# Final norm and first modulated norm in one chain of sums, in a two-stack transformer kernel

## The reference

```python
def rms_norm(x, g):
    return x * rsqrt(mean(x * x) + EPS) * g

x_end_of_first_stack:
x = rms_norm(x, final_norm)
each_layer_of_the_second_stack:
h = rms_norm_2(x, norm1) * (1.0 + scale1) + shift1
proj = h @ w_in
...
x = x + gate1 * mix
h2 = rms_norm_2(x, norm2) * (1.0 + scale2) + shift2
```

## Time and profile before

| | us |
|---|---|
| timed runs, median of 3 | 3476.75 |
| lowest and highest | 3476.37, 3479.42 |
| profiled execution | 3465.51 |
| its span | 3463.7 |
| TensorE, matmul records busy in it | 3345.2 |
| VectorE, ScalarE, GpSimd busy | 1544.0, 1214.1, 748.0 |

### The profile page before, as it was taken

The page is one execution under the profiler, slowest core; times in us unless marked ns, Lnnn a source line. Parts: engine busy times, 40 slices in busy tenths (PEclk is TensorE's granted clock), DMA queues, the critical chain, the costliest instruction groups (busy, mean ns, idle before and its releaser), DMA issues.

```text
span 3463.7 us, 40850 instructions
## 1 busy us (share of the span) xinstructions
PE 3345.2 (97%) x15998; PEld 2602.6 (75%) x15998; DVE 1544.0 (45%) x1953; ACT 1214.1 (35%) x1657; POOL 748.0 (22%) x390
## 2 busy tenths in 40 slices
PE   7999999999999999999999999989999998999999
PEld 5888776578887888876578887746788877568887
DVE  4444545545535543334543334455433345453333
ACT  4332311543323332335643323245322232552221
POOL 6677500057767740000000000030000002100000
PEclk9999999999999999999999999999999999999999
DMA  6544421145444542221033323201223331013322
GB/s 198 158 146 155 136 74 49 37 135 149 147 152 144 155 115 96 97 74 49 25 85 97 98 97 79 72 25 37 73 97 97 96 91 61 1 49 97 97 97 73
DMA packets 324130, 330.02 MB, mean 95 GB/s; under 512 B 29616, under 2 KB 284720, under 8 KB 323632
## 3 DMA queue, kind: packets, MB, share of 16 engines
q1 hardware_dynamic: 309424, 278.02, 26.0%
q0 software_dynamic: 14592, 50.44, 4.6%
HBM read 326.27 MB, written 2.15 MB: 95 GB/s over the span
## 4 chain that ended last, share of the span: by engine, by line
PE 47%; DVE 2%; ACT 1%; issue 1%; DVEq 0%; ACTq 0%
PE ps L353 18%; PE ps L569 15%; PE ps L408 2%; PE ps L549 2%; PE ps L822 1%; PE ps L849 1%; PE ps L859 1%; PE ps L489 1%; PE ps L460 1%; PE ps L377 1%; PE ps L369 1%; PE ps L1493 1%; PE ps L829 0%; ACT w_hi L302 0%; PE ps L446 0%
## 5 line engine op out<-in xcount | busy, mean ns | idle before, releaser
L306 DVE TENSOR_TENSOR w_lo<-raw,w_hi 128x2048 fp32r<-128x2048 f32 x247 | 609.2, 2466 | 573.3 <-ACT w_hi L302 572.9
L353 PE MATMUL ps<-h_hi,w_hi 128*128 128x512 f32 x2064 | 805.8, 390 | 2.6 <-DVE xT L2004 2.6
L353 PE MATMUL ps<-h_lo,w_hi 128*128 128x512 f32 x2064 | 803.1, 389 | 0.0
L353 PE MATMUL ps<-h_hi,w_lo 128*128 128x512 f32 x2064 | 803.0, 389 | 0.0
L302 ACT CAST w_hi<-raw 128x2048 fp32r<-128x2048 f32 x248 | 473.2, 1908 | 924.9 <-PE ps L353 665.6
L569 PE MATMUL ps<-a_hi,w_hi 128*128 128x512 f32 x1344 | 524.0, 390 | 10.7 <-DVE act L1977 6.2
L569 PE MATMUL ps<-a_hi,w_lo 128*128 128x512 f32 x1344 | 523.0, 389 | 0.0
L569 PE MATMUL ps<-a_lo,w_hi 128*128 128x512 f32 x1344 | 522.9, 389 | 0.0
L353 PEld LDWEIGHTS ps<-h_hi,w_hi 128*128 128x128 f32 x2064 | 387.4, 188 | 84.4 <-issue 4.3
L353 PEld LDWEIGHTS ps<-h_lo,w_hi 128*128 128x128 f32 x2064 | 387.4, 188 | 81.0 <-issue 1.0
L353 PEld LDWEIGHTS ps<-h_hi,w_lo 128*128 128x128 f32 x2064 | 387.4, 188 | 80.8
(11 more groups left out here) (284 smaller groups left out, 4006.3 us busy)
## 6 DMA issues: line engine op xcount, KB each, us to landing
raw<-in_ffn_w_in SPq DMA_DIRECT2D x176, 512.0 KB, 5.0
raw<-in_w_ff SPq DMA_DIRECT2D x128, 512.0 KB, 4.1
m_in<-in_w_mod POOLq DMA_DIRECT2D x96, 512.0 KB, 4.2
raw<-in_ffn_w_out SPq DMA_DIRECT2D x88, 512.0 KB, 4.1
raw<-in_hyb_w_in SPq DMA_DIRECT2D x28, 512.0 KB, 4.2
raw<-in_w_in SPq DMA_DIRECT2D x28, 512.0 KB, 4.7
raw<-in_sb_w_in SPq DMA_DIRECT2D x24, 512.0 KB, 4.2
raw<-in_w_out SPq DMA_DIRECT2D x16, 512.0 KB, 4.3
```

The source lines that it names most:

```text
L306: eng.tensor_tensor(w_lo[:, e % 2], raw[:, e % 2], w_hi[:, e % 2].bitcast(F32), ALU.subtract).then_inc(s["w_lo_done"], 1)
L353: mm = pe.matmul(ps[:, bank], wbuf[a][:, e % 2, at:at + P], hbuf[b][:, k], start=(k == 0 and n == 0), stop=(k == KC - 1 and n == 2))
```

## The change

The phase of the final norm is gone. The first modulated norm (layer 0) gets the number of the final norm's weights as `ph[3]` and makes both factors. ScalarE squares each chunk twice, plain into `act[:, i]` and scaled by the final weight into `act[:, 8 + i]`. `pe_two_sums` adds both sets, each into its half of the partitions of bank 1; the fold takes them apart with two columns of `col_d`. VectorE makes the first factor r into `rcol`, then r^2 times the second mean, then from this the second factor, and the product of both into `r_both`. The final weights are multiplied into `gmod`, so that the modulated norm can read the old `xT`. The product `r_both` is broadcast to bank 1 and `rcol` to bank 3. After the last low part VectorE overwrites `xT` with the final norm's result and counts it in `x_final`, on which TensorE waits in step 1 of `nsa_pre` and VectorE before the attention.

In all four modulated norms VectorE reads the broadcast factor in bank 1 and not a copy; ScalarE's copy stays for the deferred norms alone. The fillers are now 3, 16 and 9 in the joined norm, and 3, 7 and 11 in the other three, with none between the sums. The pending split is now cut in halves in the joined norm too. SyncE's wait for x counts only the updates of x.

```diff
@@ -50,7 +50,7 @@
-    ("norms", len(NORMS) * KC), ("col_d", 1), ("ret_gn", 4), ("c", KC), ("b_mod", DEPTH * 48), ("pool_scale", DEPTH * 4),
+    ("norms", len(NORMS) * KC), ("col_d", 3), ("ret_gn", 4), ("c", KC), ("b_mod", DEPTH * 48), ("pool_scale", DEPTH * 4),
...
-    phases.append(("norm", 6, "final"))
-        phases.append(("norm", 7 + 2 * l, (l, 0)))
+        phases.append(("norm", 7 + 2 * l, (l, 0), 6 if l == 0 else None))
...
@@ -372,26 +376,38 @@
             if c.norm == 1 and j == 0:
                 pe.wait_ge(s["consts_loaded"], 16)
-            pe.wait_ge(s["sq_done"], KC * (c.norm - 1) + (4, 4, 6, 8)[j])
+            pe.wait_ge(s["sq_done"], c.sq + (4, 4, 6, 8)[j])
             for o in range(2):
                 mm = pe.matmul(ps[qk_rows(o), 1], C("ones")[:, 0:HD], act[:, 2 * j + o], start=(j == 0), stop=(j == 3),
                                skip_group_check=True)
             if j == 3:
                 mm.then_inc(s["sums_done"], 1)
-
-        def pe_fold(pe, c):
+                c.sq += KC
+
+        def pe_two_sums(pe, c, i):
+
+            pe.wait_ge(s["sq_done"], c.sq + 2 * max(i, 3) + 2)
+            for o in range(2):
+                mm = pe.matmul(ps[qk_rows(o), 1], C("ones")[:, 0:HD], act[:, 8 * o + i], start=(i == 0), stop=(i == KC - 1),
+                               skip_group_check=True)
+            if i == KC - 1:
+                mm.then_inc(s["sums_done"], 1)
+                c.sq += 2 * KC
+
+        def pe_fold(pe, c, col, n):
             pe.wait_ge(s["sums_copied"], c.norm)
             for b in range(TB):
-                mm = pe.matmul(ps[:, 0, b:b + 1], rstd[:, b * P:(b + 1) * P], PR("col_d", 0),
+                mm = pe.matmul(ps[:, 0, n * b:n * b + n], rstd[:, b * P:(b + 1) * P], PR("col_d", col, n),
                                start=(b == 0), stop=(b == TB - 1), skip_group_check=True)
             mm.then_inc(s["ssq_done"], 1)
-        def pe_bcast(pe, c):
-
-            pe.wait_ge(s["norm_chain"], 6 * c.norm)
+        def pe_bcast(pe, c, of=rcol, bank=1, chain=6):
+
+            c.chain += chain
+            pe.wait_ge(s["norm_chain"], c.chain)
             for b in range(TB):
-                mm = pe.matmul(ps[:, 1, b * P:(b + 1) * P], rcol[:, b:b + 1].to_broadcast([P, P]), C("ident"),
+                mm = pe.matmul(ps[:, bank, b * P:(b + 1) * P], of[:, b:b + 1].to_broadcast([P, P]), C("ident"),
                                start=True, stop=True)
             mm.then_inc(s["bcast_done"], 1)
...
@@ -1059,17 +1075,17 @@
...
-                    sp.wait_ge(s["x_ready"], KC * sum(q[0] == "outp" or q[2:] == ("final",) for q in before))
+                    sp.wait_ge(s["x_ready"], KC * sum(q[0] == "outp" for q in before))
...
-                    sp.wait_ge(s["h_lo_done"], KC * sum(q[0] == "norm" and q[2] != "final" for q in before))
+                    sp.wait_ge(s["h_lo_done"], KC * sum(q[0] == "norm" for q in before))
...
-            sp.wait_ge(s["x_ready"], KC * sum(ph[0] == "outp" or ph[2:] == ("final",) for ph in phases))
+            sp.wait_ge(s["x_ready"], KC * sum(ph[0] == "outp" for ph in phases))
...
@@ -1249,22 +1265,26 @@
             for ph in phases:
                 if ph[0] == "norm":
                     c.norm += 1
-                    c.hnorms += ph[2] != "final"
+                    c.hnorms += 1
                     c.deferred = ph[2] is None
-                    c.fresh = ph[2] != "final"
-                    if not c.deferred:
-                        for j in range(3):
+                    c.fresh = True
+                    if ph[3] is not None:
+                        for i in range(KC):
+                            pe_two_sums(pe, c, i)
+                        keep_warm_by_weights(pe, c, 3)
+                        pe_fold(pe, c, 1, 2)
+                        keep_warm_by_weights(pe, c, 16)
+                        pe_bcast(pe, c, r_both, 1, 15)
+                        pe_bcast(pe, c, rcol, 3, 0)
+                        keep_warm_by_weights(pe, c, 9)
+                    elif not c.deferred:
+                        for j in range(4):
                             pe_sums(pe, c, j)
-                        keep_warm_by_weights(pe, c, 4)
-                        pe_sums(pe, c, 3)
                         keep_warm_by_weights(pe, c, 3)
-                        pe_fold(pe, c)
-                        keep_warm_by_weights(pe, c, 9)
+                        pe_fold(pe, c, 0, 1)
+                        keep_warm_by_weights(pe, c, 7)
                         pe_bcast(pe, c)
-                        keep_warm_by_weights(pe, c, 12)
-                    if ph[2] == "final":
-                        c.outs += 1
-                        c.order = range(KC)
+                        keep_warm_by_weights(pe, c, 11)
                 elif ph[0] == "proj":
                     pe_proj(pe, c, len(ph[2]), "T")
                 elif ph[0] == "projT":
...
@@ -1469,6 +1489,7 @@
                 elif ph[0] == "nsa_pre":
                     l, step = ph[1:]
                     if step == 1:
+                        pe.wait_ge(s["x_final"], KC)
                         pe_hn_sum(pe, c, [nbuf[:, 0], nbuf[:, 1]], 0)
                         pe.wait_ge(s["cm_w"], 80 * (l + 1))
...
@@ -1550,7 +1571,10 @@
                             eng.mul(h_hi[:, k], xT[:, k], PR("norms", ph[1] * KC + k)).then_inc(s["h_hi_done"], 1)
                         eng.activation(act[:, i], xT[:, k], ACT.Square).then_inc(s["sq_done"], 1)
-                    parts = c.pending_split and not c.deferred and ph[2] != "final"
+                        if ph[3] is not None:
+                            eng.activation(act[:, 8 + i], xT[:, k], ACT.Square, scale=PR("norms", ph[3] * KC + k)
+                                           ).then_inc(s["sq_done"], 1)
+                    parts = c.pending_split and not c.deferred
                     if c.pending_split and not parts:
                         c.pending_split()
                     c.pending_split = None
@@ -1558,23 +1582,25 @@
                     eng.copy(rstd[:, :], ps[:, 1]).then_inc(s["sums_copied"], 1)
                     if parts:
                         part_hi(eng, c.slab + 1, 0, 2)
-                    eng.wait_ge(s["norm_chain"], 6 * n + 1)
+                    eng.wait_ge(s["norm_chain"], c.chain + 1)
                     eng.activation(small[:, 52:56], small[:, 48:52], ACT.Sqrt).then_inc(s["rms_done"], 1)
+                    if ph[3] is not None:
+                        eng.wait_ge(s["norm_chain"], c.chain + 9)
+                        eng.activation(small[:, 52:56], small[:, 48:52], ACT.Sqrt).then_inc(s["rms_done"], 1)
+                    c.chain += 6 if ph[3] is None else 15
                     if parts:
                         part_hi(eng, c.slab + 1, 1, 2)
-                    eng.wait_ge(s["bcast_done"], n + 1)
-                    eng.copy(rstd[:, :], ps[:, 1]).then_inc(s["rstd_done"], 1)
-                    if ph[2] not in (None, "final"):
+                    if c.deferred:
+                        eng.wait_ge(s["bcast_done"], n + 1)
+                        eng.copy(rstd[:, :], ps[:, 1]).then_inc(s["rstd_done"], 1)
+                    else:
                         for i, k in enumerate(c.order):
                             eng.wait_ge(s["h_full"], KC * (c.hnorms - 6) + i + 1)
                             at = ph[2][0] * 48 + ph[2][1] * KC + k
                             eng.activation(h_hi[:, k], nbuf[:, i % 2], ACT.Identity, bias=mods[:, at:at + 1]
                                            ).then_inc(s["h_hi_done"], 1)
                     c.norm += 1
-                    c.hnorms += ph[2] != "final"
-                    if ph[2] == "final":
-                        c.outs += 1
-                        c.order = range(KC)
+                    c.hnorms += 1
                 elif ph[0] == "proj":
                     def work(j, e, bank, split):
                         q = c.proj + e
...
@@ -1902,40 +1928,51 @@
                     c.pending = None
                     if n == 0:
                         eng.wait_ge(s["consts_loaded"], 16)
-                    parts = c.pending_split and not c.deferred and ph[2] != "final"
+                    parts = c.pending_split and not c.deferred
                     if c.pending_split and not parts:
                         c.pending_split()
                     c.pending_split = None
-                    ms, y, u = small[:, 48:52], small[:, 52:56], small[:, 56:60]
+                    ms, y, u, ss = (small[:, 48 + 4 * a:52 + 4 * a] for a in range(4))
+
+                    def factor(mean, to):
+                        link(eng, eng.tensor_scalar(ms, mean, EPS, None, ALU.add), "norm_chain")
+                        c.roots += 1
+                        eng.wait_ge(s["rms_done"], c.roots)
+                        link(eng, eng.reciprocal(y, y), "norm_chain")
+                        link(eng, eng.tensor_tensor(u, ms, y, ALU.mult), "norm_chain")
```

(50 more changed lines are left out.)

15 lines of the change are left out of this document (10 added, 5 removed).

## The result

| | before | changed |
|---|---|---|
| timed runs, median (count) | 3476.56 (4) | 3453.47 (4) |
| lowest and highest | 3474.76, 3479.42 | 3451.62, 3460.3 |
| ratio, 95% interval | | 0.9936, 0.9919 to 0.9954 |
| profiled execution | 3465.51 | 3452.8 |
| its span | 3463.7 | 3451.0 |

The changed kernel is 0.6% faster: 23.1 us by the medians, 16 to 28 by the interval. The two profiled executions are 12.7 us apart, which is less than their changed places alone account for (17.4 us and one fall of the clock, 1.6); the table behind e1, e2 and e10 shows where the rest went.

The account below looks back on a forecast made before the run. TensorE is 97% busy, so time is won only where it waits or runs fillers, around the modulated norms. Three norms 6.4, joined norm 10.6 and clock 0.8 sum to 17.8 us off the 3476.75 median: 3459.0, range 3454.5 to 3465.5.

Parts of the forecast that it names:

- The joined norm: Final norm joined with first modulated norm: first sum to first projection 17.7 us instead of 28.3, gain 10.6 us.
- last step: In the joined norm, from VectorE's first product to the first projection matmul: 3.89 us.
- Edit 3: Three other norms: VectorE reads the broadcast in bank 1 without ScalarE's copy, gaining 0.62 us each, products no dearer.
- The moved work: Joined norm: halved weight split and VectorE's eight products making x final; 6.6 us fit into 6.91 us of VectorE idle.
- The forecast's clock: TensorE's clock falls before first projections, 1.6 us lost in one of four places, were expected no oftener in the changed kernel.
- Edits 1 and 2: Three other norms: no fillers inside the sums, 1.28 us each; seven fillers instead of nine before the broadcast, 0.23 each.
- Squares: ScalarE's squares in the joined norm: eight pairs of 0.63 + 0.72 us, ending at 2122.4, ahead of TensorE's sums.
- The cover: Joined norm: the squares stay 1.0 us ahead of TensorE, which wants the last pair at 2123.4.
- The 0.8 us for the clock: First projection behind the double norm lost 1.6 us to a lowered clock; middle between 0 and 1.6 regained.
- The clock rival: Fewer fillers let TensorE's clock fall in two to four of the four norms, 1.6 us each: 3463 to 3466; chance 0.22.
- more than summed: Rival: falls of the clock elsewhere become fewer, giving 3453 to 3456 us; chance 0.08.
- The rival of a later wait: Saving eaten by a wait for the weights of the slabs after the norm: about 3476 us; chance 0.05.

Follow-up runs that it names:

- e1: The kernel before, unchanged, run beside itself: ratio 1.0001, median 3473.7 us against 3474.0.
- e2: The changed kernel, unchanged, timed again: 3451.0 us, ratio 0.9947 to the kernel before.
- e10: The changed kernel, unchanged, timed once more beside e9 on the same chip: 3451.7 us, ratio 0.9939 to the kernel before.
- e6: The changed kernel with the old fillers (4 between the sums, 3, 9, 12) back in the three other norms: one execution, 3453.4 us.
- e5: The changed kernel without any filler in the four modulated norms: 3466.9 us, ratio 0.9976 to the kernel before.
- e9: The changed kernel with ScalarE's copy of the broadcast back in the three other norms (same kernel as e7), timed: 3462.5 us, ratio 0.9969 to before.
- e3: The joined norm alone, the three other norms in their old form: 3459.7 us, ratio 0.9962 to the kernel before.
- e4: The kernel before with only the three other norms changed (fillers 3, 7, 11, no copy), double norm kept: 3468.1 us, ratio 0.9990 to before.
- e7: The changed kernel with ScalarE's copy of the broadcast back in the three other norms: an execution of 3453.1 us.

## Why the prediction was right or wrong

**Right, by its own steps.**
- The joined norm: forecast 17.7 us, measured 17.6 in all seven profiled executions that have it with fillers and full-precision sums. Sums 7.06 forecast, 7.09 by the timeline; the two factors 3.60 and 3.58; broadcast to first product 1.33 and 2134.39 - 2133.19 = 1.20; last step 3.89 and 3.88.
- Edit 3 gave 0.62, as summed, with no dearer products.
- The moved work stayed hidden. VectorE's split followed its eight products at once (2152.61), with none of the 6.91 us of idle time left; it came about 1 us late, and TensorE's next slab hid that, as I had allowed. The high split ahead of it was as late, and is in the kernel before too (e1).
- The forecast's clock: no fall in any first projection of the changed kernel in three executions.

**Off in size.**
- Edits 1 and 2: forecast 1.51 us a norm, measured 1.63 (e6). The first is exact (4.93 to 3.65). The second was 0.35 and not 0.23: I let the gain end where the chain's result meets the load, but before, the broadcast's matmuls also stood behind fillers already loaded, and that went too (load to first product or copy 1.19 us, and not 1.33). Hence 12.0 and not 12.2 in each norm, 0.4 us in all.
- Squares: taken at 1.35 us a pair. In the changed kernel a new pair starts every 1.14 us, and the last one takes 2124.05 - 2122.82 = 1.23 from its first start to its end, because the second square starts before the first is over. The cover was 2.6 us, not 1.0. The upper bound by another line's 0.72 us was right for the duration (0.71); I had added durations where ScalarE overlaps neighbours.

**Wrong: the step from the profiled execution to the median ("I take the same 17.8 off the median"), and with it the range.** The stages gave 17.0 and the clock 0.8; the program's own gain is 17.4 by the stages and 18.4 at equal clock, within 1 us of the forecast's 17.8. But I took three timed runs within 3 us of one another for the spread of this kernel, and their median for its level. With 69 runs the spread is 17 us (3464.1 to 3481.2), and the mean 3473.1, 3.6 us below the 3476.75 I started from. The profiled execution I argued from, 11 us below that median, had been the sign of it. The rest of the miss is that the means of 69 and 16 runs lie 20.7 us apart and not 17.8. A median of four runs on either side may stray several microseconds; the measured 23.1 did, and the later ratios are 0.9947 and 0.9939 where the first was 0.9936. The range of 3454.5 to 3465.5 carried the uncertain prices of the steps, and nothing for what the clock does in stages that the change does not touch. It did not even hold to its own words: it put what a measurement can tell at 7 us, and its lower end 4.5 us below the forecast.

The 0.8 us for the clock was half of one fall, in a place where the kernel before had it in one of three profiled executions. By the mean clocks of 69 and 16 runs the clock's part is nearer 2.3, with an error of about 1. I could not settle it further.

**The rivals.** The clock rival was priced rightly at 1.6 us a fall (12.75 to 12.77 against 11.15), and the prediction set fewer fillers against shorter waits, as e5 to e9 bear out: with both taken away no projection of the changed kernel fell, with the copy back five of six did, with no fillers all four. The number measured, 3453.5, lies in the band of another rival, "more than summed", 3453 to 3456, with its chance of 0.08; the range held half of this band and not most of it. That is not the rival's mechanism shown: outside the changed places the profiled execution of the changed kernel took 4.7 us more than that of the kernel before, or 6.3 with the one fall left out, and the mean clocks are only two standard errors apart. The rival of a later wait has nothing to show: the load that ScalarE waits for is as late in the kernel before (e1), without cost.

## What to carry to other kernels

Count what an edit does to the wait of TensorE as well as to its filler work: the copy of 0.6 us in three norms cost its own length, 1.9 us, and 3.2 to 4.8 more in falls of the clock behind the longer wait. Before a range is stated, look at how far single executions of the same program lie apart and at their mean granted clock; comparing runs at equal clock told 18 us from 23 here, and the lengths of the changed stages from one execution each told the parts to 0.1 us. The whole times of the two profiled executions, 12.7 us apart, would have misled. Where two reductions follow one another and the second can be written in terms of the first, both sums can go in one pass; the cost is then the sums and one more small chain, not two rounds.

## What the runs showed of the hardware

- TensorE's wait before the first projection of a modulated norm, and how often the granted clock then fell to 1.2 GHz: 0.95 to 1.4 us, behind nine to twelve fillers, in none of the profiled executions; 1.78 to 1.79 us behind twelve, in none of nine (before, e1, e3); 1.84 us behind twelve, in one of three (before, e1, e4); 2.0 us behind eleven, in five of six (e7, e9); 2.6 to 3.9 us without fillers, in four of four (e5). At 1.84 and 2.0 us the same wait and fillers gave both outcomes. One fall cost a projection of 48 matmuls 1.6 us. The Trainium skill (TensorE: Matmul & The Clock Gate, Part 1) says that pauses bring the clock down, and the traces agree in this, that the longer waits were the ones behind which it fell.
- The mean granted clock of one program went from 0.985 to 0.991 over 69 executions, and its time with it, by 2.7 us for each 0.001.
- Two neighbouring activations of 0.62 and 0.71 us, free of waits, follow one another so that pairs start every 1.14 us: each overlaps its neighbour by 0.1 us.
- A VectorE product with one operand from the accumulators takes 748 ns, with all from the on-chip buffer 752.
